# Twelve stretches of projection instead of eighteen in each head pair of a hybrid decoder trunk

## The reference

```
for each layer:
    xn = rms_norm(h)
    layer 0: y = conv_mixers(xn)
    layer 1: q, k, v = split(xn @ w_qkv)                # 16 heads x 64
             # branches (128,1), (512,4), (2048,16): each query reads distances 0, d, .., window
             s = q.k / 8 - slope * distance             # masked where no branch reads
             att = sum over branches of softmax(s) v, merged by their softmax denominators
             y = att @ w_o
    h = h + y
    h = h + conv_ffn(rms_norm(h))
y_out = rms_norm(h) ; states, keys and values are outputs too
```

## Time and profile before

| | us |
|---|---|
| median of 3 runs | 2543.89 |
| lowest, highest | 2542.36, 2544.19 |
| the profiled execution, whole | 2548.02 |
| its span, first to last instruction | 2546.2 |

### The profile page before, as it was taken

How to read it: one execution, slowest core, us unless ns; L and a number is a source line. 1 busy time by engine, 2 the same in 40 slices (tenths; PEclk the granted TensorE clock), 3 DMA queues, 4 the chain that set the end, 5 groups by cost and what they waited for, 6 DMA issues and landing times.

```text
span 2546.2 us, 41492 instructions
## 1 busy us (share of the span) xinstructions
PE 2493.4 (98%) x17036; PEld 2371.9 (93%) x17036; DVE 1633.9 (64%) x2419; ACT 805.9 (32%) x1432; POOL 969.8 (38%) x664
## 2 busy tenths in 40 slices
PE   8999998999999999999999999998899999999998
PEld 8989998999999999998888888888899999999998
DVE  6999778666666655555555555555876666665556
ACT  5111444333333211143333333343433333331112
POOL 1000135777777422241010111123377777762223
PEclk9999999999999999999999999999999999999999
DMA  4111102455444544444455445433177777785222
GB/s 152 46 42 35 50 20 65 148 144 146 142 142 141 191 151 138 167 174 133 158 173 165 150 153 179 164 106 133 34 265 274 273 273 274 272 315 187 84 85 86
DMA packets 108667, 383.91 MB, mean 151 GB/s; under 512 B 24000, under 2 KB 44352, under 8 KB 106048
## 3 DMA queue, kind: packets, MB, share of 16 engines
q1 hardware_dynamic: 108480, 381.26, 44.8%
HBM read 339.15 MB, written 176.04 MB: 202 GB/s over the span
## 4 chain that ended last, share of the span: by engine, by line
PE 90%; DVE 5%; issue 2%; POOL 1%; ACT 1%; DMA 1%; SPq 0%; DVEq 0%; POOLq 0%; ACTq 0%
PE reg L997 29%; PE reg L856 19%; PE reg L1115 10%; PE reg L823 9%; PE ob L997 3%; PE reg L1137 3%; PE reg L1091 3%; PE reg L1151 3%; PE reg L929 2%; PE reg L836 2%; PE reg L1062 1%; PE reg L1207 1%; PE reg L1194 1%; DVE xo L2169 1%; PE ob L903 1%
## 5 line engine op out<-in xcount | busy, mean ns | idle before, releaser
L997 PE MATMUL reg<-xo,wq 128*128 128x352 f32 x5280 | 862.8, 323 | 18.6 <-DVE tmp L2248 6.6
L997 PEld LDWEIGHTS reg<-xo,wq 128*128 128x128 f32 x5280 | 851.7, 189 | 23.4 <-DVE tmp L2248 7.2
L856 PE MATMUL reg<-hid,w_sp 128*128 128x352 f32 x3024 | 485.3, 322 | 0.0
L856 PEld LDWEIGHTS reg<-hid,w_sp 128*128 128x128 f32 x3024 | 485.0, 188 | 0.0
L518 POOL TENSOR_TENSOR w_sp<-w_raw,w_sp 128x1024 fp32r<-128x1024 f32 x63 | 174.2, 2767 | 712.8 <-ACT w_sp L513 692.3
L1979 DVE TENSOR_TENSOR h<-reg,h 128x1056 f32<-128x1056 f32 x192 | 241.3, 1257 | 235.7 <-PE reg L856 211.7
L1833 POOL TENSOR_TENSOR wq<-wqr,wq 128x512 fp32r<-128x512 f32 x168 | 239.6, 1435 | 216.1 <-DVE wqr L2208 134.5
L1115 PE MATMUL reg<-xs,w_sp 128*128 128x352 f32 x1701 | 309.7, 331 | 0.0
L1833 POOL TENSOR_TENSOR wq<-w_raw,wq 128x512 fp32r<-128x512 f32 x168 | 265.5, 1592 | 59.5 <-ACT wq L1373 59.4
L1115 PEld LDWEIGHTS reg<-xs,w_sp 128*128 128x128 f32 x1701 | 270.8, 189 | 13.9 <-issue 12.6
L823 PE MATMUL reg<-xs,w_sp 128*128 128x352 f32 x1512 | 245.1, 324 | 5.6 <-DVE h L1979 5.6
(11 more groups left out here) (272 smaller groups left out, 3090.2 us busy)
## 6 DMA issues: line engine op xcount, KB each, us to landing
w_raw<-in_wstream SPq DMA_DIRECT2D x192, 512.0 KB, 4.3
out_sv<-in_cache_v SPq DMA_DIRECT2D x16, 4088.0 KB, 16.8
out_sk<-in_cache_k SPq DMA_DIRECT2D x16, 4088.0 KB, 17.2
kvr<-in_kva SPq DMA_DIRECT2D x16, 2048.0 KB, 9.4
kvr<-in_kvb SPq DMA_DIRECT2D x16, 1536.0 KB, 7.0
hid_spill<-tmp SPq DMA_DIRECT2D x44, 528.0 KB, 5.4
hraw<-hid_spill SPq DMA_DIRECT2D x44, 528.0 KB, 4.5
wt<-in_wtab SPq DMA_DIRECT2D x16, 512.0 KB, 4.0
```

The lines of the kernel that those rows point to most:

```text
L856: mm = nc.tensor.matmul(out[:, t, :], w[:, wh, kk * 512 + m * P:kk * 512 + (m + 1) * P], hid[:, par_g, kk, xh, t * TS:(t + 1) * TS], start ...
L997: mm = nc.tensor.matmul(out, w[:, wh, k * P:(k + 1) * P], xo[:, o, 1 - xh if o == X_T3 else xh, k, :], start=(first and k == 0 and wh + xh ...
```

## The change

The 18 fillers of a pair keep their content and their order, but their places change. Two tables name, for each group, the fillers ahead of the low turn (`LEAD`) and those behind the high turn (`COVER`), the first row of each for pairs 0 to 6, the second for the last pair. No filler stands any more between the low turn and what follows it. In a pair there are 6 stretches ahead of low turns and 6 behind high turns, of one or two fillers each. DVE's `take_third` of a third follows at the start of the next group or behind the `norm` of this one. ACT's split of one weight unit of the last pair moves up from the end of group 3 to before its low turn, and the copy of `wo7` is chained.

```
+LEAD = (((0, 1), (3,), (6, 7), (9,), (12, 13), (15,)), ((), (2, 3), (6, 7), (10, 11), (14,), (16,)))
+COVER = (((2,), (4, 5), (8,), (10, 11), (14,), (16, 17)), ((0, 1), (4, 5), (8, 9), (12, 13), (15,), (17,)))
...
                 for g in range(NGR):
+                    for f in LEAD[pr.last][g]:
+                        filler(f)
                     turn(g, "lo")
-                    filler(3 * g)
                     if g == 0:
                         turn_values()
...
                     turn(g, "hi")
-                    filler(3 * g + 1)
+                    for f in COVER[pr.last][g]:
+                        filler(f)
                     weigh(g)
                     if g in SAMPLE_AT:
                         sample_phase(SAMPLE_AT[g])
-                    filler(3 * g + 2)
...
+                    if pr.last and g == 3:
+                        split_hi(act, U_WO + 3, done=9 * NPAIR + 5)
...
                 for g in range(NGR):
+                    if g == 0:
+                        next_third(-1)
+                    elif COVER[pr.last][g - 1][-1] % 2 == 1:
+                        next_third(COVER[pr.last][g - 1][-1] // 2)
                     for hh in range(2):
                         norm(g, hh)
-                    if g % 2 == 0:
-                        next_third(3 * g // 2 - 1)
+                    if LEAD[pr.last][g] and LEAD[pr.last][g][-1] % 2 == 1:
+                        next_third(LEAD[pr.last][g][-1] // 2)
                     turned(g, "lo")
-                    if g % 2 == 1:
-                        next_third(3 * g // 2)
...
-                    if g % 2 == 0:
-                        next_third((3 * g + 1) // 2)
                     if g < 2:
                         sample_scores(g)
```

More of the change, by code:

```diff
@@ L1759, in pair @@
                         act.wait_ge(ta_full, pr.n(ta("phase", 2) + 1, NTA))
-                        nc.scalar.activation(wo7[:, :, :], w_sp[:, U_WO % 3, :, (KD - 1) * P:KD * P].bitcast(F32), ACT.Copy)
-                    if pr.last and g == 3:
-                        split_hi(act, U_WO + 3, done=9 * NPAIR + 5)
+                        chain(nc.scalar.activation(wo7[:, :, :], w_sp[:, U_WO % 3, :, (KD - 1) * P:KD * P].bitcast(F32),
+                                                   ACT.Copy))
             first = Pair(0)
```

## The result

| | before | after | |
|---|---|---|---|
| median, first chip (4 runs each) | 2544.04 us | 2577.52 us | ratio 1.012, 95% interval 1.0104 to 1.0136 |
| lowest, highest | 2542.36, 2548.22 | 2570.24, 2579.44 | |
| median, second chip (17 and 5 runs) | 2547.77 us | 2574.91 us | ratio 1.0107, interval 1.0092 to 1.0121 |
| span of the profiled execution | 2546.2 us | 2568.4 us | |

The change costs 33.5 us by the first pair of medians and 27.1 us by the second; the forecast was 24.4 us. The profiled execution of after was the fastest of its four, 7.3 us under their median. I first show the waits that the forecast named, then what it left out.

A forecast was written before the change was run, and what follows sets the result against it. PE alone was taken to bound the attention stage; 19.4 (pairs 1 to 7) - 0.9 (first) + 0.7 (seventh) + 5.2 (last) = 24.4 us, median 2543.9 to 2568.3 us; range 2553 to 2578 us, 8 in 10 or a little more.

The forecast's parts named there:

- a late load or weight split: Rival (6%): PE's moved order makes a sample-phase load or weight split late; one microsecond more per pair, 2577 us and more.
- PE bounds the stage: Attention stage, middle pair: PE busy 71.90 of 72.00 us, so any wait PE has to make is paid in full.
- Changes of work: On PE, fillers joined to others: 0.06 us less each, six times per pair, 0.36 us saved.
- Turn behind turn: Values, weights, sample outputs directly behind a low turn: PE waits for DVE's copy, 0.55, 0.55 and 0.70, sum 1.80 us per pair.
- Third behind phase 2: Filler 6, opening third 3 behind phase 2: PE waits 1.65 us for DVE's take_third; bounds 1.5 and 1.8.
- Low turn of group 2: With two fillers ahead, its wait for norm goes: 1.19 to 0.87 us, -0.32 us per pair.
- First pair: At the stage's start, fillers 0 and 1 start 0.9 us earlier, -0.9 us; the half clock is paid on fillers.
- Seventh pair: PE arrives earlier at the high turn, relative to ACT's copy of the sample outputs: a wait of 0.7 us.
- Last pair: Late thirds, low turn 0, turn behind turn and the moved last filler, less gains: 5.2 us more, bounds 2 and 8.
- Nothing outside the stage: Stages ahead of 1140 us and behind the attention must not differ.
- The clock, nothing: Longest new wait, 1.65 us, is shorter than waits of 3.16 and 2.22 us in the traces; nothing counted for the clock.
- The rival that put a fall into every pair: Rival (5%): the clock falls in each pair, 2.5 us per pair, 20 us for eight pairs, 2588 us.

The follow-up runs named there:

- take_early: Changed kernel, same PE order, but DVE takes the third ahead of the sample scores (groups 0, 1) and the addition to so (group 4): 2555.69 us, ratio 1.0029.
- wait_1us: Kernel before plus one wait per pair: ahead of the filler behind phase 2, PE waits for DVE's maximum of the sample scores: 2554.06 us, ratio 1.0021.
- again: The changed kernel run once more, unaltered, on the second chip: median 2574.91 us.
- cover_turns: Changed kernel with fillers from ahead of the low turn put between it and values, weights and sample outputs: 2603.84 us, ratio 1.0219.
- both: Changed kernel with the edits of take_early and cover_turns together: 2583.32 us, ratio 1.0137.

## Why the prediction was right, and what it left out

The direction and the places were right; the time was 9 us too low by the first chip's median. That median, 2577.5 us, lies inside the stated range of 2553 to 2578 by 0.5 us, and 0.5 us above the 2562 to 2577 that the forecast itself was given. The range reached to 2578 for another reason, a late load or weight split that costs a microsecond per pair, and neither profile of the changed kernel shows such a wait in the pairs. So that the number fell inside it is in part luck. By its steps:

**PE bounds the stage.** Right: every wait showed up in the time, in both directions (after, take_early, wait_1us).

**Changes of work, 0.06 us each.** Small, as forecast. A middle pair without a fall takes 75.51 us from high turn 5 to high turn 5, 72.54 before: +2.97 for 2.77 forecast. The two waits below are 1.74 and 1.93 us; less the 0.32 us at low turn 2 that makes 3.35, so the six changes gave back 0.38 us, where 0.36 was forecast.

**Turn behind turn, 1.80 us per pair.** Measured by starts, 0.61 + 0.62 at values and outputs, and 0.70 at the weights whose low turn has 0.79 us before: 1.93 us.

**Third behind phase 2, 1.65 us.** From phase 2's last pair of matmuls to the filler it was 0.25 us before and is 1.99 us: 1.74 us. take_early removed it alone.

**Low turn of group 2, -0.32 us.** Right in the sum, wrong in what was to show it. By starts it went from 1.19 to 0.96 us and not to 0.87: scores follow it now, and ahead of scores a turn takes 0.97 us, which the sum has among its changes of work.

**First pair, -0.9 us.** Too small: to high turn 5 of the first pair the stage took 76.62 us before and 79.31 after, of which 1.58 is a fall, so +1.1 where 1.9 was forecast. The starting fillers paid for the low clock with 1.6 us (24 matmuls in 5.46 for 3.89 us), where the old order paid about 2.5 us on a turn and a filler.

**Seventh pair, 0.7 us.** Right: the high turn waited 0.76 us for ACT.

**Last pair, 5.2 us.** From high turn 5 of the seventh pair (1652.51 before, 1674.89 after) to the last row it took 74.4 us before and 79.5 after: 5.1 us. That is closer than its estimates deserved. The three waits for thirds were 1.5, 1.6 and 1.1 us, as forecast; but the 1.4 us at the pair's start was 0.4 us for `norm` and 0.3 us for ACT, and the 0.9 us ahead of the last row of the output projection was in no term.

Together the stage grew by 24.7 to 25.0 us without the falls, for 24.4 forecast.

**Nothing outside the stage.** Ahead of 1140 us the profile of after is 0.7 us shorter than that of before, and behind the attention 5.3 us. The forecast had said that these parts would not differ. By the profile of wait_1us, which has the old order and the faster pace, this comes and goes between executions.

**The clock, nothing.** This is the step that failed. I took the two rows of waits of 3.16 and 2.22 us as a border and reasoned that 1.65 us, shorter than both, was safe. A single row that shows no fall does not show that none can come. In the profiles of after and again the clock fell behind 3 of 18 such waits, with cover_turns behind 7 of 27, at 1.58 us a fall. By the 7 of 27 that is 2.3 falls or 3.7 us for the nine waits of an execution, an estimate from three profiles. The rival that put a fall into every pair had the right mechanism and too large a size. With the 3.7 us the sum would have been about 28.1 us, which lies inside the intervals of both chips (26.5 to 34.6 and 23.4 to 30.8 us) and still 5 us under the first chip's median. How much of that median's 33.5 us is more falls, the pace of the second ConvFFN or chance among four runs stays open.

## What to carry to other kernels

Work that fills gaps on the bounding engine has several jobs at once: it covers a copy out of a PSUM tile, it covers a softmax on other engines, and it needs its own tile back. List for each stretch what its successor waits for before moving it, and count how much filler lies on each of those chains; joining stretches saved 0.06 us each, a lost cover cost 0.6 to 1.7 us. Where a moved instruction needs something from another engine, look at the place in that engine's program: one line moved ahead of an unrelated wait on DVE was worth 19 us here.

## What the runs showed of the hardware that was not expected

The clock of TensorE can fall from 2.4 to 1.2 GHz behind a single wait of 1.58 us in a stage that is otherwise full: 7 of 27 waits for `take_third` and 7 of 29 waits of 1.53 to 1.66 us for `norm` (cover_turns and both), against 0 of 8 at 1.06 us and 3 of 8 at 2.25 us. A wait of 3.46 us in the second ConvFFN had 1.00 behind it in five of the nine profiles, before among them, and 0.50 in again, take_early, cover_turns and wait_1us. The same wait in the same kernel is followed by a fall in one pair and not in the next, and in another pair in another execution. A fall costs 1.4 us on 12 matmuls and 1.6 us on 24 matmuls of 352 columns. A VectorE operation on 128 by 352 elements took 0.57 us where a GpSimd operation of 2.40 us began 0.41 us after it, and 2.65 us where one of 2.62 us had begun 0.35 us before it. Long rows of matmuls of 352 columns ran at 312 in 50 us in some executions and 317 in others, both at a granted clock of 1.00.
